# Column sums and spreads replaced by row products and transfers in a gated delta mixer; order of three engines changed

## The reference

```
qkv = silu(causal_dwconv(cat[q, k, v], conv_w))       # 12 tiles of 128 channels: q 0-3, k 4-7, v 8-11
q, k = l2norm(q), l2norm(k)                           # x * rsqrt(sum(x*x) + EPS), per head of 128 channels
beta = sigmoid(b); g = -exp(a_log) * softplus(a + dt_bias)      # (512, 4 heads)
gc = cumsum(g in each chunk)
decay = where(tril, exp(gc[i] - gc[j]), 0)
L = where(strict, (k * beta) @ k.T * decay, 0);  T = inverse(I + L)
attn = where(tril, (q @ k.T) * decay, 0)
# scan over chunks: v_new = u - w @ S; o = (q*exp(gc)) @ S + attn @ v_new; S = ...
o = o * rsqrt(mean(o*o, axis=-1) + EPS) * o_norm_g * silu(z)
```

## Time and profile before

| | |
|---|---|
| median of 3 runs | 1998.6 us (1996.96 to 1999.41) |
| profiled execution, its own time | 1994.3 us |
| its span in the trace | 1992.4 us |
| TensorE busy | 1971.0 us, 99% |
| VectorE busy | 1210.4 us, 61% |
| ScalarE busy | 824.4 us, 41% |
| GpSimd busy | 16.2 us |
| granted TensorE clock over the span | 0.999 of 2.4 GHz |

### The profile page before, as it was taken

The page is one execution under the profiler, slowest core; times in us unless marked ns, Lnnn a source line. Parts: engine busy times, 40 slices in busy tenths (PEclk is TensorE's granted clock), DMA queues, the critical chain, the costliest instruction groups (busy, mean ns, idle before and its releaser), DMA issues. The chain is left out here.

```text
span 1992.4 us, 26556 instructions
## 1 busy us (share of the span) xinstructions
PE 1971.0 (99%) x10434; PEld 1616.0 (81%) x10434; DVE 1210.4 (61%) x1708; ACT 824.4 (41%) x1241; POOL 16.2 (1%) x31
## 2 busy tenths in 40 slices
PE   9999999999999999999999999998999999999998
PEld 7888888888677888788888888887988788888887
DVE  6676565688899545654434367886564456544534
ACT  6554343434777353532223255532454442222222
POOL 0000000000000000000000000010000000000000
PEclk9999999999999999999999999999999999999999
DMA  7998897454333552333333233211143323323231
GB/s 253 301 300 291 288 287 254 169 186 165 127 106 127 190 201 85 117 96 100 93 103 96 82 102 95 85 53 30 43 141 113 106 85 96 106 95 96 95 100 69
DMA packets 80922, 275.42 MB, mean 138 GB/s; under 512 B 9216, under 2 KB 11776, under 8 KB 80800
## 3 DMA queue, kind: packets, MB, share of 16 engines
q1 hardware_dynamic: 79648, 272.36, 41.7%
q10 hardware_dynamic: 1152, 1.38, 0.2%
HBM read 240.61 MB, written 32.51 MB: 137 GB/s over the span
## 5 line engine op out<-in xcount | busy, mean ns | idle before, releaser
L342 PE MATMUL ps<-Hh,whi 128*128 128x512 f32 x1456 | 573.1, 394 | 4.2 <-ACT P L1278 2.2
L346 PE MATMUL ps<-Hh,wlo 128*128 128x512 f32 x1456 | 567.3, 390 | 0.5 <-DVE wlo L1768 0.5
L343 PE MATMUL ps<-Hl,whi 128*128 128x512 f32 x1456 | 566.7, 389 | 0.0
L1093 ACT CAST whi<-raw 128x1024 fp32r<-128x1024 f32 (+3 forms) x352 | 350.2, 999 | 383.6 <-PE ps L346 344.9
L1768 DVE TENSOR_TENSOR wlo<-raw,whi 128x1024 fp32r<-128x1024 f32 (+3 forms) x294 | 338.8, 1157 | 181.2 <-ACT whi L1093 174.4
L342 PEld LDWEIGHTS ps<-Hh,whi 128*128 128x128 f32 x1456 | 273.3, 188 | 68.3 <-issue 6.0
L346 PEld LDWEIGHTS ps<-Hh,wlo 128*128 128x128 f32 x1456 | 273.3, 188 | 58.7 <-DVE wlo L1768 1.1
L343 PEld LDWEIGHTS ps<-Hl,whi 128*128 128x128 f32 x1456 | 273.4, 188 | 56.4 <-issue 1.2
L1884 DVE SCALAR_TENSOR_TENSOR cacc<-upad,gains,cacc 128x512 f32<-128x512 f32 x232 | 160.2, 745 | 0.8
L1834 DVE SCALAR_TENSOR_TENSOR x<-ps,x 128x512 f32<-128x512 f32 x79 | 54.6, 691 | 155.1 <-PE ps L346 155.1
L1810 DVE TENSOR_TENSOR scr<-ps,Rt 128x512 f32<-128x512 f32 x92 | 63.2, 687 | 54.8 <-PE ps L346 40.2
(11 more groups left out here) (384 smaller groups left out, 2806.2 us busy)
## 6 DMA issues: line engine op xcount, KB each, us to landing
raw<-in_w SPq DMA_DIRECT2D x369, 512.0 KB, 4.0
low_parts<-lo SPq DMA_DIRECT2D x58, 512.0 KB, 4.7
wlo<-low_parts SPq DMA_DIRECT2D x58, 512.0 KB, 3.4
raw<-in_w SPq DMA_DIRECT2D x16, 384.0 KB, 3.1
raw<-in_w SPq DMA_DIRECT2D x17, 256.0 KB, 2.6
out<-y SPq DMA_DIRECT2D x8, 256.0 KB, 2.0
x<-in_x SPq DMA_DIRECT2D x5, 256.0 KB, 6.2
raw<-in_w SPq DMA_DIRECT2D x8, 128.0 KB, 2.0
```

What stands on the lines that cost most here:

```text
L342: e.matmul(out, h[:, kk, :], a, start=part != "last" and k + kk == 0, stop=False)
L343: e.matmul(out, h[:, kk, :], c, start=False, stop=False)
L346: ins = e.matmul(out, lo[:, kk, :], a, start=False, stop=done)
L1093: e.copy(whi[i % WS][:, 0:n], raw[i % RAWS][:, 0:n]).then_inc(*act.tick("whi", ("whi", i)))
```

## The change

Five parts, all but the last in the second block's mixer.

1. **Norms of keys and queries.** `columns` and `spread` of the 8 tiles go; each gets one `mean_row` (128x128 of ones by 128x512 squares). ScalarE reads the sums from PSUM with Ln into SBUF (`long(i)`, a tile of `aT` for the keys and of `TT` for the queries), and then does Exp in place. VectorE's reciprocals go and `unit_qk` reads SBUF. The clearing of `TT` on GpSimd moves behind the last `unit_qk`.
2. **Rows of the chunks.** The four pairs of K = 4 products go. SP's queue writes beta and gc (2 x 8 KB) to DRAM and reads each head's row back onto 128 partitions, into `Xm` and `LT` (8 transfers of 256 KB), between loads of weight pieces. ScalarE's order in a chunk becomes Exp first, then Relu and Exp; VectorE first multiplies `LT` by `kk`, then by the decay.
3. **Norms of the scan's outputs.** The four `columns` + `spread` become `mean_row` + `root_row` (Ln and Exp in PSUM); `first_half(5)` moves ahead of `second_half(0)`.
4. **Orders.** VectorE does `unit_qk(0, 1)` before pool tile 3, `unit_qk(2, 3)` before conv 9, the scaling of conv 11 and `left32(1)` inside `chunk(3)`, `left32(2)` before the pieces due after `zg` 0 and before conv 11. ScalarE does the squares 0 and 3 earlier and conv 11 after `zgate(0)`.
5. **Second SwiGLU network's first weights.** The casts and subtractions of its third and fourth piece move from behind the squares of `e` to before and among them.

```diff
+        long = lambda i: (aT if i >= 4 else TT)[:, i % 4, :, :].rearrange("p b c -> p (b c)")
...
-            def qk_columns(*tiles):
+            def qk_rows(*tiles):
                 for i in tiles:
-                    pe.wait_ge("qk_sq", i)
-                    columns(("qk", i), scr[3 + i % 3], ps(("cols", "k" if i >= 4 else "q")), 4, 4 * (i % 4))
+                    mean_row(("qk", i), "qk_sq", i, src=scr[3 + i % 3], c=128)
...
             conv4(0)
-            take(("cols", "k"), pin=True)
-            qk_columns(4, 5)
+            qk_rows(4, 5)
             conv4(1)
-            qk_columns(6, 7)
-            ring.append(bank_of["cols", "k"])
+            qk_rows(6, 7)
...
-            k_spread(4, 5)
             other("pi", 0)
-            k_spread(6, 7)
+            qk_rows(0, 1)
             other("pi", 1)
+            qk_rows(2)
...
             ins.then_inc(*pe.tick("sums", ("bt",)))
-            take(("cols", "q"), pin=True)
-            qk_columns(0)
             other("pi", 2)
-            qk_columns(1, 2)
-            p3 = begun(("pi", 3), "w_in_2", 384, Hh, Hl, "mix2")
-            p3(range(4))
-            qk_columns(3)
-            ring.append(bank_of["cols", "q"])
-            p3(range(4, 8))
+            qk_rows(3)
+            other("pi", 3)
...
             def chunk(h):
-                bg = take(("bg", h))
-                e.matmul(bg[:, :], cg[32:36, 32 + h:33 + h].to_broadcast([4, 128]), grow, start=True, stop=True).then_inc(*pe.tick("rows", ("bg", h)))
-                bb = take(("bb", h))
-                e.matmul(bb[:, :], cg[0:4, h:h + 1].to_broadcast([4, 128]), brow, start=True, stop=True).then_inc(*pe.tick("rows", ("bb", h)))
...
             conv4(8)
-            q_spread(0, 1)
...
             conv4(9)
-            q_spread(2, 3)
...
-            def on_columns(c):
-                b = take(("cols", ("on", c)))
-                pe.wait_ge("on_sq", c)
-                columns(("on", c), scr[c % 2], b)
...
                     ins.then_inc(*pe.tick("rule", ("wS", c)))
-                    on_columns(c - 1)
+                    on_row(c - 1)
...
                 ins.then_inc(*pe.tick("rule", ("o", c)))
-                if c:
-                    on_spread(c - 1)
             first_half(2)
-            on_columns(3)
+            on_row(3)
             first_half(3)
-            on_spread(3)
             first_half(4)
+            first_half(5)
             for j in range(8):
-                if j >= 5:
+                if j >= 6:
...
             load("c2", c2[:, :], io["c2"])
+            weights(ends["cv", 2] + 4)
+            sp.wait_ge("brow")
+            e.dma_start(rows_d[0:2048].rearrange("(h t) -> h t", h=4), rows[0:4, 0, :]).then_inc(*sp.tick("rows_b", ("rows_d", 0), by=16))
+            sp.wait_ge("ab_g")
+            e.dma_start(rows_d[2048:4096].rearrange("(h t) -> h t", h=4), rows[32:36, 0, :]).then_inc(*sp.tick("rows_g", ("rows_d", 1), by=16))
+            weights(ends["cv", 2] + 5)
+            sp.wait_ge("rows_d", 0)
+            sp.wait_ge("rows_d", 1)
+            for h in range(4):
+                e.dma_start(Xm[:, h, :, :].rearrange("p b c -> p (b c)"), rows_d[2048 + 512 * h:2560 + 512 * h].partition_broadcast(128)).then_inc(
+                    *sp.tick(f"bg{h}", ("bg", h), by=16))
+                e.dma_start(LT[:, h, :, :].rearrange("p b c -> p (b c)"), rows_d[512 * h:512 + 512 * h].partition_broadcast(128)).then_inc(
+                    *sp.tick(f"bb{h}", ("bb", h), by=16))
+                weights(ends["cv", 2] + 6 + h)
...
             norm_row("f2", "mix")
+            weights(ends["pl", 7] + 3)
...
                     act.wait_ge("spread", "f2")
+                if j == 5:
+                    weights(ends["pl", 7] + 4)
...
-            def qk_deviation(key, last):
-                act.wait_ge("cols", ("qk", last))
-                e.activation(cols(("sd", key), 16), ps(("cols", key))[:, 0:16], AF.Sqrt, bias=epsc, scale=1.0).then_inc(
-                    *act.tick("sd", ("sd", key), ("free", ("cols", key))))
+            def qk_log(*tiles):
...
+                for i in tiles:
+                    act.wait_ge("spread", ("qk", i))
+                    if i == 0:
+                        act.wait_ge("qkv0")
+                    e.activation(long(i), ps(("R", ("qk", i)))[:, :], AF.Ln, bias=epsc, scale=1.0).then_inc(
+                        *act.tick("sd", ("ln", ("qk", i)), ("free", ("R", ("qk", i)))))
...
+            def qk_root(*tiles):
...
+                for i in tiles:
+                    act.wait_ge("ln", ("qk", i))
+                    e.activation(long(i), long(i), AF.Exp, scale=-0.5).then_inc(*act.tick("R", ("R", ("qk", i))))
...
             conv4(0)
+            qk_square(0)
+            qk_log(4, 5, 6, 7)
             after(("cv", 2))
-            qk_square(0)
-            qk_deviation("k", 7)
+            qk_root(4, 5, 6, 7)
...
             conv4(3)
+            qk_square(3)
...
             after(("pi", 1))
+            qk_log(0, 1)
...
             after(("pi", 2))
-            qk_square(3)
+            qk_log(2, 3)
             after(("pi", 3))
-            qk_deviation("q", 3)
+            qk_root(0, 1, 2, 3)
...
                 act.wait_ge("bg", h)
+                if h >= 2:
+                    act.wait_ge("pl", 3)
+                e.activation(flat(Tm, h), flat(Xm, h), AF.Exp).then_inc(*act.tick("decay", ("eg", h)))
                 act.wait_ge("tc1")
+                act.wait_ge("eg", h)
...
                     g = 16 + 4 * blk + h
-                    ins = e.activation(Xm[:, h, blk, :], ps(("bg", h))[:, 128 * blk:128 * blk + 128], AF.Relu, bias=tc[:, g:g + 1], scale=-1.0)
+                    ins = e.activation(Xm[:, h, blk, :], Xm[:, h, blk, :], AF.Relu, bias=tc[:, g:g + 1], scale=-1.0)
...
                 e.activation(flat(Xm, h), flat(Xm, h), AF.Exp, scale=-1.0).then_inc(*act.tick("decay", ("decay", h)))
-                act.wait_ge("pl", 3)
-                e.activation(flat(Tm, h), ps(("bg", h))[:, :], AF.Exp).then_inc(*act.tick("decay", ("eg", h), ("free", ("bg", h))))
...
             after(("cv", 11))
-            conv4(11)
...
             after(("zg", 0))
+            conv4(11)
...
             def on_high(c):
-                deviation(("on", c), 4, 1.0 / 128)
+                root_row(("on", c), 1.0 / 128)
...
             for j in range(1, 8):
+                if j in (2, 6):
+                    weights(ends["pl", 7] + (3 if j == 2 else 4))
...
             conv4_in(1)
-            reciprocal("k", 16)
...
                 dve.wait_ge("kk", h)
-                e.tensor_tensor(L3, dt_, ps(("kk", h))[:, :], MUL).then_inc(*dve.tick("chunk", ("L0", h), ("free", ("kk", h))))
                 dve.wait_ge("bb", h)
+                e.tensor_tensor(L3, L3, ps(("kk", h))[:, :], MUL).then_inc(*dve.tick("chunk", ("L0", h), ("free", ("kk", h))))
                 dve.wait_ge("L0", h)
-                e.tensor_tensor(L3, L3, ps(("bb", h))[:, :], MUL).then_inc(*dve.tick("chunk", ("L", h), ("free", ("bb", h))))
+                dve.wait_ge("decay", h)
+                e.tensor_tensor(L3, L3, dt_, MUL).then_inc(*dve.tick("chunk", ("L", h)))
...
                     first32()
+                    conv4_in(11)
...
                 e.tensor_tensor(a3, dt_, ps(("kq", h))[:, :], MUL).then_inc(*dve.tick("chunk", ("a0", h), ("free", ("kq", h))))
+                if h == 3:
+                    left32(1)
...
             after(("pi", 3))
-            reciprocal("q", 16)
+            unit_qk(0)
+            unit_qk(1)
...
             conv4(8)
-            unit_qk(0)
-            unit_qk(1)
...
             after(("cv", 8))
+            unit_qk(2)
+            unit_qk(3)
...
             conv4(9)
-            unit_qk(2)
-            unit_qk(3)
...
-            conv4_in(11)
             after(("cv", 11))
-            left32(1)
-            conv4(11)
...
             zgate(0)
+            left32(2)
             after(("zg", 0))
-            left32(2)
+            conv4(11)
...
                                        op0=MUL, op1=MUL).then_inc(*dve.tick("on", ("on_z", c), ("free", ("o", c))))
-                dve.wait_ge("spread", ("on", c))
+                dve.wait_ge("R", ("on", c))
...
             e.memset(up[:, :, 0:16], 0.0).then_inc(*pool.tick("zero", ("up1",)))
-            e.memset(TT[:, :, :, :], 0.0).then_inc(*pool.tick("zero", ("TTz",)))
...
                 pool.wait_ge("cv", 3)
-                pool.wait_ge("TTz")
...
             pool.wait_ge("a0", 3)
+            pool.wait_ge("qk", 3)
+            pool.wait_ge("SL", 2)
+            e.memset(TT[:, :, :, :], 0.0).then_inc(*pool.tick("zero", ("TTz",)))
```

30 lines of the change are left out of this document (11 added, 19 removed).

## The result

The changed kernel takes 1984.35 us (median of 4 runs, 1983.71 to 1986.57) where the kernel before takes 1997.96 (4 runs, 1996.96 to 1999.41). The ratio is 0.993, with a 95% interval of 0.9917 to 0.9942, so it is 13.6 us faster. The forecast was 1985.3. The number is right; one of its terms isn't, and this study is mostly about that one.

What follows compares the result with a forecast made beforehand. TensorE, busy 99% of the span, bounds the kernel, with VectorE becoming the mixer's bound after the change. Gains of 8.3 + 3.1 + 1.9 = 13.3 us against the median 1998.6 give 1985.3 us, range 1978.5 to 1992.5.

Steps and rivals of the forecast that it cites:

- The slots: TensorE work removed: 7.5 us at key and query norms, 4.2 at row products, 3.8 in the scan, together 15.5.
- the scan's term: Scan: 3.8 us of TensorE slots go, 0.7 is given back at one chunk for VectorE's `vn`: 3.1 us gained.
- ScalarE's delay of VectorE: Keys: Ln and Exp ahead of pool casts move VectorE's following work by 2.6 us, the keys' end to 1288.4.
- VectorE becomes the bound: Mixer, keys to `zg` 0: VectorE's 47.5 us of work makes TensorE wait about 4.4; gain 7.2 us, not 11.7.
- The inversion: Behind `zg` 0: `left32` waits of 2.0 us go, new waits of 1.1 and 1.0 come; 1.1 us net gain.
- an unnamed gap of 1.2 us: Inversion: a TensorE gap of about 1.2 us was to swallow one of the new waits.
- VectorE is late: Mixer; denies the rival that VectorE is never late, full saving of 19.4 us, 1979.2 us, chance 0.17.
- casts aren't late for TensorE: Keys, queries and scan; denies the rival that casts come late, gain about 6 us smaller, 1991.5 us, chance 0.19.
- the transfers are hidden: Chunk rows; denies the rival that broadcasts hold up weights, 27.5 us lost, 2012.8 us, chance 0.06.
- the gain is not small: Mixer and inversion; denies the rival that little changes, gain 2 to 4 us, about 1996, chance 0.08.
- The second SwiGLU's start: Start of the second SwiGLU: waits of 1.2 us for a cast and 0.7 for a subtraction go, 1.9 us.

Runs made afterwards that it cites:

- e2: Changed kernel with ScalarE's casts for pool tiles 0 and 1 put back ahead of the keys' Ln and Exp: 1980.74 us, ratio 0.9921.
- e1b: Changed kernel with two repeated 128x512 additions on VectorE (1.5 us together) ahead of the piece of `zg` 0: 1984.52 us, ratio 0.9932.
- e4: Changed kernel with the chunks' rows made by the K = 4 products again, without writes and broadcasts, old ScalarE and VectorE chunk code: 1982.15 us, ratio 0.9929.
- e3: Changed kernel with 14 unused 128x512 products (3.2 us) on TensorE ahead of the first product of `zg` 0: 1982.66 us, ratio 0.9931.
- e8: e7 with 12 unused 128x512 products (2.7 us) ahead of the first product of `zg` 1: 1975.85 us, ratio 0.9895.
- e12: Changed kernel with 12 unused products (2.7 us) ahead of the first product of `zg` 1: 1983.24 us, ratio 0.9928.
- the second trace: The kernel before, unchanged, traced once more: 1997.52 us (one run), span 1995.6 us.
- e5: Kernel before with only the casts and subtractions of the second SwiGLU's third and fourth piece moved: 1996.11 us, ratio 0.9988.
- e6: Changed kernel with the scan's four norms by `columns` and `spread` again and `first_half(5)` behind `second_half(0)`: 1986.93 us, ratio 0.9940.
- e7: e2 with VectorE's convolution of conv 10 moved behind `right32(1)` and ScalarE's casts for `zg` 1 and 2 earlier: 1979.79 us, ratio 0.9902.
- e11: e7 with real products of `zg` 1 moved ahead of `left_product(2)` and `zg` 2 begun behind `right_product(2)`: 1974.93 us, ratio 0.9887.
- e9: e2 with 10 unused 128x512 products (2.3 us) ahead of the first product of `zg` 0: 1980.71 us, ratio 0.9918.

## Why the prediction was right, and where it wasn't

**The slots.** Right, within a microsecond. Up to `zg` 0 the gain of 7.7 us and the 4.8 of new waits make 12.5, where 11.7 were counted; the scan's term, 3.1, measured 2.7.

**ScalarE's delay of VectorE.** Right, and nearly to the tenth. On the changed trace's own axis, 2.1 us ahead, the pool piece is made at 1269.64 + 2.1 = 1271.7 (forecast 1271.6) and the stretch of VectorE's work begins at 1288.0 (forecast 1288.4). e2 shows that this delay costs 3 us at left(1); by its timed runs the whole is 1.8 to 3.6, which they can't part from none.

**VectorE becomes the bound.** Right. Its work was put at 47.5 us and takes 47.3; the piece of `zg` 0 is ready at 1333.22 + 2.1 = 1335.3 (forecast 1335.9); TensorE waits 4.8 us in two places (forecast 4.4). e1b moves this place by what is added, 1.4 us, and e4 shows the other side, that 4.2 us of slots are worth nothing there.

**The inversion.** Wrong: "2.0 - 1.1 - 1.0 + 1.2 = 1.1 net" measured -3.0. The waits for `left32` went, as said, and of the 2.1 us that were to come for `right32(2)` and the piece of `zg` 1 only 0.35 did. But the step took the wait at `zg` 0 to cost its own length. TensorE comes out of it at half its clock, another 1.4 us; e3 gives 1.0 of it back by keeping TensorE busy. And it took an unnamed gap of 1.2 us to be swallowed. That was misread: both gaps of the earlier trace rows lie behind `left_product(3)`, outside this stretch, and the one inside it, 1.08 us, isn't among those rows. In the changed trace it is 2.0 us, with a second fall of 1.6 us behind it. That the change made it longer isn't shown: the unchanged kernel has 1.08 there in one trace and 2.15 in the other. e8 and e12 show smaller gaps with 12 wide products more in front, one trace each.

**Why the sum came out at all.** 13.3 was forecast, the traces give 10.5 and the medians 13.6. The missing 3 us are made up on the other side: I took the profiled execution's path for the usual one, and only corrected its length by its distance from the median. That distance, 4.3 us, can be such a gap and such a fall in the kernel before; the second trace shows 3.2 of it. The changed kernel's four runs were all at 0.995 to 0.997 and those of the kernel before mostly at 0.996 to 0.998, while its first trace has no fall here. That the two errors have the same size and cancel in the median is luck: the forecast knew of neither. In the words of the forecast's rivals, none of the four was at work: VectorE is late, casts aren't late for TensorE, the transfers are hidden, and the gain is not small.

**The second SwiGLU's start.** 1.9 forecast, 2.1 in the trace, 2.35 by e5's medians.

**What stays open.** That the unnamed gaps are TensorE short of instructions is an inference: they stand at fixed places in its list of instructions, e8 and e12 show that wide work put in front is free there, and the transfers of instructions come one in 4 us, but no row says what the sequencer waited for. What sets a gap's length, which changes from one execution to the next, is open. So is when the clock falls behind one: a gap of 2.0 us has a fall behind it in the changed kernel and none in e6, at the same place, and one of 1.55 has it in e3 and not in e8. No variant was traced twice, so which of the differences behind left(1) are the edit's and which are chance isn't known; a second and third trace of the changed kernel and of e7 would tell.

## What to carry to other kernels

Taking slots off the bounding engine pays only up to the next engine's feet: sum the second engine's busy time over the stretch, and if it fills more than the bound engine's new length, move its work out of the stretch first. A long wait on TensorE costs more than its length, since the products behind it may run at half the clock; it is worth breaking up, and another order of work that is there anyway can do it, as in e11. And one trace is one execution: if its own time stands off the median, a second trace shows how much of a difference between two kernels is there without any change.

## What the hardware showed

- The granted clock fell to its lower level behind all of TensorE's idle stretches from 2.15 us on in this part of the traces: waits of 3.67 (e6), 3.66 (changed), 3.50 (e12), 2.62 (e1b) and 2.42 (e2), gaps of 2.55 (e7), 2.18 (e5, e9) and 2.15 (second trace before). Among shorter ones the length doesn't decide: it fell behind 2.00 (changed), 1.60 (e7), 1.58 (e5) and 1.55 (e3), and didn't behind 2.04 (e1b), 2.00 (e6), 1.73 (e1b, e2), 1.59 (e1b) and 1.55 (e8). A fall took in four to eight products of 128x512 at 0.427 us in place of 0.227.
- It fell once without a wait: in e12's trace seven products after the twelve tiny K = 4 products of `bt`, which took 1.9 us, run at 0.427. It cost nothing there, VectorE being the bound.
- 2.7 us of useless products cost nothing in two kernels (e8, e12), and 14 of them removed a fall of the clock (e3).
- Unnamed gaps of TensorE stand at fixed places in its list of instructions, 254 and 256 records apart in the changed kernel and in the kernel before, and 12 products more in front move them by 12 records.
- Reading a 2 KB row onto 128 partitions, 256 KB, took 4.1 and 4.7 us to land, two at a time, without delaying 512 KB weight loads (3.6 us median in both traces).
